# A block of transformer layers on one core: constants multiplied in TensorE's waits, and the gating branch of an attention stage spread between the heads

## What is computed

```python
# block 1, two layers; mod = silu(c) @ ada_w + ada_b gives shifts, scales and gates g1, g2
h = rmsnorm(x, norm_mix) * (1 + sc1) + sh1
x = x + g1 * mixer(h)            # mixer: h @ w_in -> u, v, q, k, values
#   spatial gating: gelu(u) * (W_masked @ rmsnorm(gelu(v)) + b), 8 heads of 64
#   stick-breaking attention, 8 heads of 64:
#     a[t,s] = exp(log_sigmoid(z_ts) + sum_{s<j<t} log_sigmoid(-z_tj)), s < t
#   the halves joined, a norm each, @ w_out
h = rmsnorm(x, norm_ffn) * (1 + sc2) + sh2
x = x + g2 * peer_ffn(h)         # top 16 of 128x128 product keys, gathered rows of two tables
# block 2: ffn, (pool | gated conv 31 wide), ffn;  ffn, sparse attention of 16 heads, ffn
x = x + 0.5 * (silu(h @ w_gate) * (h @ w_up)) @ w_down        # h = rms_norm(x)
# block 3: ffn, (mamba2 | block attention) gated, ffn, with a layer norm after each
```

## Time and profile before

| | us |
|---|---|
| three runs | 3917.23, 3916.43, 3915.93 |
| median | 3916.43 |
| the profiled execution | 3912.03 |
| its span | 3910.2 |
| mean granted TensorE clock | 0.952 of full |
| TensorE busy | 3252.5 |
| VectorE busy | 2156.8 |
| ScalarE busy | 1014.4 |
| GpSimd busy | 1033.1 |

### The profile page before, as it was taken

One profiled execution on the slowest core, in us unless ns is written; L12 is line 12 of the kernel. 1 busy time (PEld: TensorE's weight loads), 2 busy tenths in 40 slices (PEclk: granted clock), 3 DMA queues, 4 the chain that ended last, 5 costly groups with the idle time before them and its releaser, 6 DMA issues. The chain is left out here.

```text
span 3910.2 us, 34931 instructions
## 1 busy us (share of the span) xinstructions
PE 3252.5 (83%) x12416; PEld 2229.5 (57%) x12416; DVE 2156.8 (55%) x3737; ACT 1014.4 (26%) x1597; POOL 1033.1 (26%) x1092
## 2 busy tenths in 40 slices
PE   5897567778887577777998999999998989878798
PEld 3673222223664222223876687876687878767686
DVE  5578766544559766645544455523445435555654
ACT  0211111111112111112432344412343312434333
POOL 0027777764016777764000000000000000200000
PEclk9799899999899899999998999998999989989999
DMA  9369999999549999999651455542455534243453
GB/s 365 142 226 368 409 409 409 409 404 369 229 152 344 409 409 409 409 409 338 195 167 65 157 187 168 187 146 86 130 185 173 185 124 147 75 154 128 151 183 118
DMA packets 402041, 951.19 MB, mean 243 GB/s; under 512 B 30652, under 2 KB 171488, under 8 KB 401632
## 3 DMA queue, kind: packets, MB, share of 16 engines
q0 software_dynamic: 147456, 536.94, 34.9%
q1 hardware_dynamic: 245088, 397.09, 30.3%
q10 hardware_dynamic: 9344, 15.22, 1.1%
HBM read 948.06 MB, written 1.07 MB: 243 GB/s over the span
## 5 line engine op out<-in xcount | busy, mean ns | idle before, releaser
L1463 PE MATMUL PS<-v_rows,xn 128*128 128x512 f32 x1944 | 910.4, 612 | 360.9 <-DMA v_rows<-in_peer_v_dram,peer_ids 350.8
L1463 PEld LDWEIGHTS PS<-v_rows,xn 128*128 128x128 f32 x1944 | 356.4, 193 | 913.8 <-issue 553.6
L1544 DVE CUSTOM_DVE_ANT_0 u_rows<-u_rows,PS 128x1024 f32<-128x1024 f32 x512 | 621.8, 1220 | 365.9 <-DMA u_rows<-in_peer_u_dram,peer_ids 338.1
L760 DVE TENSOR_TENSOR ring_lo<-ring,ring_hi 128x2048 fp32r<-128x2048 f32 x198 | 452.9, 2292 | 260.3 <-ACT ring_hi L699 259.8
L1618 POOL DMA_INDIRECT u_rows<-in_peer_u_dram,peer_ids x512 | 484.7, 947 | 268.9 <-issue 145.2
L1618 POOL DMA_INDIRECT v_rows<-in_peer_v_dram,peer_ids x512 | 487.5, 952 | 169.3 <-issue 144.3
L699 ACT CAST ring_hi<-ring 128x2048 fp32r<-128x2048 f32 x198 | 376.7, 1912 | 287.1 <-PE PS L616 156.2
L616 PE MATMUL PS<-ring_hi,hT_hi 128*128 128x512 f32 x1056 | 420.2, 398 | 16.6 <-DVE hT_lo L800 12.1
L616 PE MATMUL PS<-ring_hi,hT_lo 128*128 128x512 f32 x1056 | 414.3, 392 | 0.0
L616 PE MATMUL PS<-ring_lo,hT_hi 128*128 128x512 f32 x1056 | 413.8, 392 | 0.0
L442 PE MATMUL PS<-hT,ring 128*128 128x256 f32 x1664 | 366.9, 382 | 1.2 <-DVE hT L406 1.2
(11 more groups left out here) (400 smaller groups left out, 3708.3 us busy)
## 6 DMA issues: line engine op xcount, KB each, us to landing
ring<-in_ffn_w_gate_dram SPq DMA_DIRECT2D x132, 512.0 KB, 3.9
ring<-in_ffn_w_up_dram SPq DMA_DIRECT2D x132, 512.0 KB, 4.9
ring<-in_ffn_w_down_dram SPq DMA_DIRECT2D x66, 1024.0 KB, 4.8
ring<-in_w_in_dram SPq DMA_DIRECT2D x64, 1024.0 KB, 5.1
ada_ring<-in_ada_w_dram SPq DMA_DIRECT2D x96, 512.0 KB, 8.6
ring<-in_peer_wq_dram SPq DMA_DIRECT2D x16, 1024.0 KB, 7.3
ring<-in_c_w_in_dram SPq DMA_DIRECT2D x14, 1024.0 KB, 5.0
ring<-in_w_out_dram SPq DMA_DIRECT2D x8, 1024.0 KB, 12.2
```

The source lines that it names most:

```text
L760: nc.vector.tensor_tensor(halves(c)[1], slot, halves(c)[0], ALU.subtract).then_inc(S.w_lo, 1)
L1463: ins = nc.tensor.matmul(self.PS[:, 2 * b + h, :], diag[:, r % NDIAG, :], rowsV[:, m % VRING, h * BANK:(h + 1) * BANK], start=(n % (slots ...
L1544: ins = nc.vector.tensor_tensor_reduce(rowsU[:, m % URING, :], rowsU[:, m % URING, :], H[b], 1.0, 0.0, ALU.mult, ALU.add, dots[:, e:e + 1])
```

## The change

`keep_clock(bank, count)` is new: count matmuls of the constant ones (128 x 128) with the constant identity into a bank that is free at that time. Nobody reads the result, and no semaphore is raised or waited for. It is put into 27 places of TensorE's row, in its waits and at the ends of stages; counts go from 4 to 64, and over the whole program, with the stages that run twice or more, there are 746 calls. A float32 matmul stands as two records in the trace, so a call is two records.

In the attention stage of the mixer the gating branch on DVE no longer stands as a block ahead of the heads and in head 1. Its pieces follow `exponents(h)` of heads 0 to 4, one a head (`gate_step`), and `gate_outputs` follows head 6 instead of head 4; every `exponents` has a drain behind it. TensorE's 16 matmuls stand behind `values(4)` (before: `values(2)`). The three sums of gates stand together in head 7, into banks 0 and 1, 6, and 4 and 5; the semaphore gate_out is gone.

`keep_clock`, the norm of a stage, the end of `ada_start`, and `ffn` (behind its transposes, and around the last `down`):

```diff
+    def keep_clock(self, bank, count):
+
+        for _ in range(count):
+            self.nc.tensor.matmul(self.PS[:, bank, 0:P], self.ones, self.ident, start=True, stop=True, skip_group_check=True)
+
-    def norm_tensor(self, pe, S, src=None):
+    def norm_tensor(self, pe, S, src=None, lead=17, pause=4):
...
+        self.keep_clock(2, lead)
         for b in range(NB):
             pe.wait_ge(S.n_xn, b + 1)
...
                 ins.then_inc(S.n_tr, 1)
+        self.keep_clock(2, pause)
...
                 self.sum_columns(self.PS[:, 0, KT:2 * KT], 1).then_inc(S.columns, 1)
+                self.keep_clock(1, 14)
...
+                self.keep_clock(3, 7 if layer_norm else 14)
                 up(pe, 0, None, 0, 0, head=True)
...
                 turn(pe, s, None, s % 2)
+                self.keep_clock(3 - 2 * (s % 2), 5)
                 down(pe, s, last, None)
+                self.keep_clock(0, after)
```

The mixer's attention, TensorE:

```diff
                         sums(h)
+                        if h == 0:
+                            self.keep_clock(2, 4)
                         if h >= 1:
                             values(h - 1)
-                        if h == 3:
+                        if h == 5:
                             pe.wait_ge(S.wT_out, 1)
                             pe.wait_ge(S.v_hat, 1)
...
-                        if h == 5:
+                        if h == 7:
+                            pe.wait_ge(S.expo, 6)
+                            self.sum_spread(0, 5)
+                            pe.wait_ge(S.expo, 7)
+                            for i, v in enumerate((3, 4)):
+                                ins = self.sum_columns(self.PS[:, 6, i * KT:(i + 1) * KT], v)
+                            ins.then_inc(S.ada_sum, 1)
                             pe.wait_ge(S.gated_out, 1)
                             self.sum_spread(4, 2).then_inc(S.gate_sum, 1)
-                        if h == 7:
-                            pe.wait_ge(S.expo, 5)
-                            for i, v in enumerate((3, 4)):
-                                self.sum_columns(self.PS[:, 0, i * KT:(i + 1) * KT], v)
-                            pe.wait_ge(S.gate_out, 1)
-                            self.sum_spread(4, 5).then_inc(S.ada_sum, 1)
                     values(HEADS - 1)
```

The same stage, DVE (`gate_step` holds the instructions of `gate_inputs` and `gate_scale`):

```diff
+                    def gate_step(h):
+                        if h == 0:
+                            nc.vector.tensor_tensor(sq[:], V[:], V[:], ALU.mult)
+                        elif h == 1:
+                            nc.vector.tensor_reduce(vms[:], v3(sq[:]), AX.X, ALU.add)
...
+                        elif h == 2:
+                            ve.wait_ge(S.wT, 1)
+                            nc.vector.tensor_copy(wT[:].rearrange("p (g h) n -> p g (h n)", g=2), self.PS[:, 4:6, :])
...
+                        elif h == 3:
+                            ve.wait_ge(S.v_rstd, 1)
...
+                        elif h == 4:
+                            ve.wait_ge(side, 64)
...
                     keeps(0)
                     keeps(1)
-                    gate_inputs()
                     for h in range(HEADS):
-                        if h == 1:
-                            ve.wait_ge(side, 64)
-                            gate_scale()
                         if h + 2 < HEADS:
                             keeps(h + 2)
                         exponents(h)
-                        if h == 4:
+                        nc.vector.drain()
+                        gate_step(h)
+                        if h == 6:
                             gate_outputs()
-                        if h == 6:
-                            ve.wait_ge(S.gate_sum, 1)
-                            residual_gate(0).then_inc(S.gate_out, 1)
                     ve.wait_ge(S.ada_sum, 1)
-                    residual_gate(1)
...
+                    residual_gate(1, 0)
...
+                    ve.wait_ge(S.gate_sum, 1)
+                    residual_gate(0, 4)
```

More of the change, by code:

```diff
@@ L580, in _, with ffn @@
                 self.sum_columns(self.PS[:, 0, KT:2 * KT], 1).then_inc(S.columns, 1)
-    def ffn(self, name, gain=None, layer_norm=None):
+                self.keep_clock(1, 14)
+    def ffn(self, name, gain=None, layer_norm=None, after=4):
         nc = self.nc
@@ L883, in layer_norm_scale, with final_norm @@
         nc.vector.scalar_tensor_tensor(self.X[:, b, :], self.xn[:, b, :], self.rstd[:, b:b + 1], lnp[:, 1, :], ALU.mult, ALU.add)
-    def final_norm(self, gain):
+    def final_norm(self, gain, lead):
         nc = self.nc
@@ L890, in final_norm, with _ @@
             landed = nc.alloc_semaphore("gain_landed_" + str(self.n_stage))
+            @block.tensor
+            def _(pe):
+                self.keep_clock(0, lead)
             @block.scalar
@@ L984, in _ @@
                     self.norm_gpsimd(pool, S)
-            with ExitStack() as inner, self.stage("scores sp keep summed expo att pv wT wT_out v_ms v_rstd v_hat gated gated_out gate_sum gate_out ada_sum",
+            with ExitStack() as inner, self.stage("scores sp keep summed expo att pv wT wT_out v_ms v_rstd v_hat gated gated_out gate_sum ada_sum",
                             side=0 if l == 0 else None) as (block, S):
@@ L1176, in _ @@
                 def _(pe):
-                    self.norm_tensor(pe, S, src=Y)
+                    self.norm_tensor(pe, S, src=Y, lead=19)
                     pe.wait_ge(S.n_hT, self.N_HT)
@@ L1414, in back @@
                         ins.then_inc(S.back, 1)
-                    self.norm_tensor(pe, S)
+                    self.norm_tensor(pe, S, pause=0)
                     pe.wait_ge(side, 32)
@@ L1884, in _ @@
                     scores(h + AHEAD - 1)
+                if h == 0:
+                    self.keep_clock(4, 6)
                 turn(h)
@@ L1888, in _ @@
             values(heads - 1)
+            self.keep_clock(3, 4)
         @block.vector
@@ L2170, in _ @@
                         turn(i)
+                    self.keep_clock(7, 40)
                 @block.scalar
@@ L2544, in _ @@
                 def _(pe):
+                    self.keep_clock(7, 24)
                     self.project_halves(pe, S, ["F"] * 2 + ["T"] * 2, hh[:, :, 0, :], hh[:, :, 1, :], KT, both)
+                    self.keep_clock(7, 17)
                 @block.scalar
@@ L2705, in build @@
                 self.ffn(f"ffn2_{l}", self.col("ffn2_norm_2")[:, cols])
-            self.final_norm(a["final_norm_2"])
-            self.ffn("ffn1_3", layer_norm=(a["ln1_g_3"], a["ln1_b_3"]))
+            self.final_norm(a["final_norm_2"], 33)
+            self.ffn("ffn1_3", layer_norm=(a["ln1_g_3"], a["ln1_b_3"]), after=64)
             self.hybrid()
```

45 lines of the change are left out of this document (25 added, 20 removed).

## The result

The changed kernel takes 3869.24 us (median of 4 runs, 3864.91 to 3871.07), the kernel before 3916.83 (4 runs, 3915.93 to 3924.09): 47.6 us less by the medians (3869.24 / 3916.83 = 0.9878).

A forecast was written before the change was run, and what follows sets the result against it. TensorE bounds the kernel, busy 3252.5 of 3910.2 us, partly at 1.2 GHz. Clock 43.1 plus mixers' attention 8.8 less 6 for overrunning calls is 45.9 off 3912.03: 3866.1, plus 4.4 carried over to the median, 3870 us; range 3846 to 3897.

The forecast's parts named there:

- the block attention: Block attention and what stands before it, 64.34 us at clock 0.90: a gain of 3.0 us, 6.4 at most.
- sparse attention: Its 23.85 us piece, TensorE busy throughout at clock 0.57: a gain of 7.7 us, bounds 4 and 10.2.
- the four FFN stages: Four of six FFN stages show a slow stretch; at full clock each gains 1.62 us, 6.5 in all.
- the end of the first stage: 14 calls there start at 1.2 GHz, 6.0 us long; next stage 1.7 us late at least, 6.0 at most; 1.7 taken.
- the mixers' attention: Two layers, 53.71 and 49.05 us, become 47 each between 41 fast and 56 slow: a gain of 8.8 us.
- the norms' term: Transposes after norms run at full clock instead of 1.2 GHz: a gain of 7.7 us.
- seven runs at 1.1: Seven of eight runs of transposes after norms gain 1.1 us each, taken between 0.9 and 1.7; the first stays slow.
- Rival 1: Both mixers' attentions fall to 1.2 GHz, 112 us in place of 94: 3888 us; chance 0.12.
- Rival 2: The clock rises, but DVE, ACT or transfers are late and hide half of the 43.1 us: 3892 us; chance 0.09.
- Rival 3: Transposes don't count as work for the clock, so FFN and norm terms, 14.2 us, go: 3884 us; chance 0.05.
- Rival 4: Products of constants don't hold the clock; calls take 0.43 us or more and overrun by 118 us: 4030; chance 0.04.
- Rival 5: Calls run but the clock falls in remaining pauses as before; only the attention's reordering is left, near 3905 us; chance 0.05.

The follow-up runs named there:

- second trace: The changed kernel itself run once more, unaltered, beside other kernels; 3869.44 us, ratio 0.9879 to the kernel before.
- order_only: The changed kernel with every keep_clock call empty, so only the mixers' attention's new order is left; ratio 0.9957 to before on its chip.
- calls_only: The changed kernel with the mixers' attention's old order; meant to keep all calls, it had only 622 of the 746; ratio 0.9933 to before.
- columns_early: The changed kernel with sum_columns moved out of the mixers' attention's tail into the heads, behind values(2) and ahead of values(4); 3872.35 us, ratio 0.9873.
- calls_as_transposes: The changed kernel with every call made of two transposes of the constant in place of one float32 product; ratio 0.9869 to before.

## Why the prediction was right, step by step

The forecast was 3870 us, the measurement 3869.24. Its working was less exact than that. In the trace 41.0 us went where 45.9 were forecast, and the profiled run stood 1.8 above the median where I had carried over a profiled run 4.4 below it: the two errors cancel, and that the forecast hit to 1 us is luck. By terms the attention gave 6.0 us more than forecast, the norms 5 less in the stages' lengths and the block attention 2 less, and effects that stood in no term (the scan, the first final norm, two FFN stages) took 5.6. The second trace lies 44.9 below before.

**Right, in the first trace, to some half a microsecond**: ab_out 2.1 (forecast 2.1), sparse attention 7.6 (7.7), ssm_in 3.4 (4.0), ssm_z 2.5 (2.7), ssm_out 2.2 (2.4), c_in's products 3.3 (3.2), the four FFN stages 6.1 (6.5), the end of the first stage 1.7 (1.7). The pool chain gave 2.8 and 3.6 in the two traces (3.8). Not all of this is firm: ssm_z gained 2.3 to 2.5 in five of the eleven traces with calls and 0.8 to 1.2 in the other six, the last FFN stage gained its 1.6 in six and nothing in five, and c_in was 3.1 us shorter in order_only without any call. For the sparse attention the size is right and it did run at full clock, but calls_only got there without the calls of that stage. The 14 calls (28 records) behind L316, which I priced at 6.0, and the next stage's first work on DVE:

```profile
44.41 5.79 PE L386 MATMUL PS<-cst 128*128 128x128 f32 x28
...
50.62 0.17 DVE L982 TENSOR_TENSOR mod<-first_mod,prm 128x16 f32<-128x16 f32 x1 [13.21 <-PEq L349]
```

The calls went at 1.2 GHz all along, 5.79 us for 14, and the next stage began 1.46 us later than in the earlier trace rows. The calls were 0.23 us at full clock (0.22 to 0.24).

**Right in mechanism, wrong in size**: the mixers' attention, 14.8 us (12.2 in the second trace) for 8.8. The pace of heads is 3.81 us at full clock, held by stick_log as forecast:

```profile
1036.31 0.70 PE L1026 MATMUL PS<-stick_qT,stick_kT 64*128 64x256 f32 x2 [1.20 <-DVE stick_log L1120]
...
1040.12 0.70 PE L1026 MATMUL PS<-stick_qT,stick_kT 64*128 64x256 f32 x2 [1.20 <-DVE stick_log L1120]
...
1053.80 4.43 PE L316 MATMUL PS<-cst,ada_sums 128*128 128x1 f32 x32
...
1058.09 3.76 PE L323 MATMUL PS<-ada_sums,cst 128*128 128x512 f32 x4
```

A head begins 3.81 us after the other, and TensorE waits 1.20 of them for stick_log. I had taken 47 us a layer between 41 and 56; the twelve layers with exactly this order and these calls inside it, in six traces, have a median of 45.3 and lie between 41.1 and 47.3. The share of the slow end was overrated, and the bounds held. The two last rows are the tail: `sum_columns` has 4.43 us and the last sum_spread 3.76 where the one ahead has 1.94, because the clock falls in the run of one-column products.

**Wrong**: the norms' term, 7.7 us, of which 2.7 came in the first trace outside PEER (mix_in of layer 1 1.0, ab_in 1.5, c_in 1.3, mix_out minus 1.1). In PEER the products begin 0.2 us later in the first layer and 1.4 earlier in the second, but its two stages are no shorter for it, 1441.8 us in sum against 1441.6. The failed step is "seven runs at 1.1". The runs are all at full clock, but ahead of three of them (the two mix_out and the first PEER) the lead itself ran slow behind a slow end, and came out later than the scaled tile: in mix_out it ended 7.1 us after the barrier, and its transposes began at 6.95 instead of 4.82. And the first mix_in had its end set by another engine. What stood at its end in the trace of the changed kernel:

```profile
124.54 6.78 SPq L275 DMA_DIRECT2D ring<-in_peer_wq_dram  x2
...
132.21 1.23 PE L1026 MATMUL PS<-stick_qT,stick_kT 64*128 64x256 f32 x4 [2.94 <-PEq L349]
```

SyncE issues two transfers for the weights of PEER's queries from 124.54 on, for 6.78 us (5.32 before, from 124.58), and the barrier waits for it: TensorE's next work is at 132.21, though it was done at 129.27. The 1.3 us that the products of mix_in start earlier are lost in it.

**Wrong too**: the block attention and its parts, 3.0 forecast and about 1 come. The window's clock rose to 0.97, but TensorE had waited there for others, and does so now. And three effects that I had not in the sum: 1.7 us in the scan; 1.5 in the first final norm (6.3 to 6.6 us in seven traces and 7.7 to 8.0 in five, by when its gain lands, so most likely no effect of the change; in calls_only it is 9.1, because its 25 calls ran slow, for 8.67 us, and held the barrier); and the FFN stages that begin with transposes and had no slow stretch: the first has now

```profile
1833.77 2.81 PE L686 MATMUL PS<-cst,X 128*128 128x128 f32 x16 [2.18 <-PEq L349]
...
1836.37 4.11 PE L386 MATMUL PS<-cst 128*128 128x128 f32 x28
```

transposes partly and calls partly at 1.2 GHz, 1.1 us late (not in the second trace).

**The rivals.** Rival 1 (both attentions low) didn't come in the changed kernel, but one layer of it did in order_only and columns_early, at 52.8 and 53.8 us. Rival 2 held for the last window only. Rival 3 is out by calls_as_transposes. Rival 4's mechanism, calls at 0.43 us, exists in single places (the first stage, the leads behind the attention) and cost some 3 us in sum (1.5 in the first stage, 1.2 in the two mix_out and 0.2 in PEER by the start of their products), not 118. Rival 5 is out: by the ratios order_only gives a third of what the changed kernel gives, and the mean clock of the changed kernel's trace is 0.978 against 0.952.

## What to carry to other kernels

Where TensorE's clock falls when it waits, as in this kernel, work that nobody reads can pay, if it fits the wait and joins work on both sides; what is beyond the room costs its full price at once (14.9 us for ten more calls in eight places), and behind a slow end the filler runs slow too and overruns. Look first which engine waits for TensorE in the slow stretch: a slow stretch at a stage's start that DVE hides is worth leaving, since removing it may put it on the chain. Cut the long wait itself if the order allows it: with the old order the filler made the two attention stages 11 us slower in the one trace taken.

## What the runs showed of the hardware that I had not expected

A layer of eight heads is in one of two regimes. At full clock TensorE waits 1.2 of 3.81 us in each head and the clock mostly stays. At 1.2 GHz it is busy all of 4.75 us, and in the nine layers in which the clock fell between 6 and 11 us after the barrier it stayed low for 17 to 38 us (8.7 to 46.2 in columns_early); stretches that begin at 20 us or later among the heads last from 3 to 17. The same instructions took 41.1 to 47.3 us with the calls and 42.1 and 52.8 without them. Why continuous work at the low level doesn't raise the clock there, where transposes in an FFN's start did, none of the runs tells. A run of 32 one-column products from full clock ended slow in both layers of the changed kernel's first trace (4.43 us, with the next four records at 3.76 for 1.94). Eleven traces have this run in two layers each: the clock fell within it, or up to 1.2 us behind its end, in 20 of the 22, and in two it didn't fall at all. And the issue of two DMAs on SyncE took between 5.3 and 6.8 us at the same place, which I can't explain by these runs either.
